# The z projection of a hybrid decoder layer computed with tokens as the stationary operand, and its silu turned by TensorE

## The reference, cut to what matters

```python
z, xbc, dt_raw, q, k, v, gate_logits = jnp.split(u @ w_in, IN_SPLITS, axis=-1)
xbc = silu(causal_dwconv(xbc, ssm_conv_w, ssm_conv_b))
xs, bm, cm = split(xbc)                       # 4096, 8*128, 8*128 channels
y = ssd_chunked(xs, dt, a, bm, cm) + d_skip * xs
y = y.reshape(b, s, 8, 512) * silu(z).reshape(b, s, 8, 512)
y = y * rsqrt(mean(y * y, axis=-1) + eps)     # one mean per group of 512 channels
```

## Time and profile before

| | |
|---|---|
| median of three runs | 1941.22 us |
| the profiled execution's own time | 1941.04 us |
| its span, first to last instruction | 1938.9 us |
| TensorE (PE) busy | 1921.0 us, 99% |
| weight loads (PEld) busy | 1634.6 us, 84% |
| VectorE (DVE) busy | 1265.0 us, 65% |
| ScalarE (ACT) busy | 1084.6 us, 56% |
| DMA queues, share of 16 engines | 61% |
| granted TensorE clock | 0.999 of full |

### The profile page before, as it was taken

The page is one execution under the profiler, slowest core; times in us unless marked ns, Lnnn a source line. Parts: engine busy times, 40 slices in busy tenths (PEclk is TensorE's granted clock), DMA queues, the critical chain, the costliest instruction groups (busy, mean ns, idle before and its releaser), DMA issues.

```text
span 1938.9 us, 28968 instructions
## 1 busy us (share of the span) xinstructions
PE 1921.0 (99%) x10273; PEld 1634.6 (84%) x10273; DVE 1265.0 (65%) x1534; ACT 1084.6 (56%) x1474; POOL 33.5 (2%) x80
## 2 busy tenths in 40 slices
PE   8999999999999999999999999999999999999998
PEld 7888888888887878888888888888888888888886
DVE  6777788777868975544454555776776666744454
ACT  6567756676556764444344445666666666534443
POOL 1000000000000100000000000000000000000000
PEclk9999999999999999999999999999999999999999
DMA  7766676666654437666666565666666656665564
GB/s 222 209 186 173 196 205 176 192 174 204 197 154 135 133 122 217 193 188 196 195 193 195 175 228 195 197 187 186 191 189 194 187 184 187 192 200 192 194 195 141
DMA packets 294134, 362.05 MB, mean 187 GB/s; under 512 B 10864, under 2 KB 217776, under 8 KB 292656
## 3 DMA queue, kind: packets, MB, share of 16 engines
q1 hardware_dynamic: 294064, 361.12, 61.0%
HBM read 358.91 MB, written 2.16 MB: 186 GB/s over the span
## 4 chain that ended last, share of the span: by engine, by line
PE 97%; DVE 1%; ACT 1%; issue 0%; DMA 0%; DVEq 0%; SPq 0%; POOLq 0%; POOL 0%; ACTq 0%
PE ps L1373 35%; PE ps L1375 18%; PE ps L1358 13%; PE ps L1359 13%; PE ps L1360 13%; PE ps L1561 1%; PE ps L1489 1%; PE ps L1502 1%; PE ps L1513 0%; PE ps L1562 0%; PE ps L1550 0%; PE ps L1406 0%; DMA par<-params 0%; DVE lo L847 0%; ACT hi L437 0%
## 5 line engine op out<-in xcount | busy, mean ns | idle before, releaser
L847 DVE TENSOR_TENSOR lo<-raw,hi 128x1024 fp32r<-128x1024 f32 x658 | 801.6, 1224 | 520.7 <-ACT hi L437 515.1
L1373 PE MATMUL ps<-uHL,hi 128*128 128x512 f32 x2960 | 1042.3, 396 | 1.3 <-DVE uHL L859 1.0
L437 ACT ACTIVATE hi<-raw 128x1024 fp32r<-128x1024 f32 x658 | 688.9, 1055 | 519.3 <-PE ps L1360 386.0
L1375 PE MATMUL ps<-uHL,lo 128*128 128x256 f32 x2960 | 829.1, 280 | 0.0
L1373 PEld LDWEIGHTS ps<-uHL,hi 128*128 128x128 f32 x2960 | 554.9, 187 | 131.7 <-issue 5.0
L1375 PEld LDWEIGHTS ps<-uHL,lo 128*128 128x128 f32 x2960 | 559.9, 189 | 0.1
L1360 PE MATMUL ps<-hi,aL 128*128 128x512 f32 x384 | 149.6, 390 | 0.0
L1360 PE MATMUL ps<-hi,hL 128*128 128x512 f32 x352 | 137.0, 389 | 0.0
L1359 PE MATMUL ps<-lo,hH 128*128 128x512 f32 x352 | 137.0, 389 | 0.0
L1358 PE MATMUL ps<-hi,hH 128*128 128x512 f32 x352 | 137.0, 389 | 0.0
L442 ACT ACTIVATE hb<-ps 128x512 f32<-128x512 f32 x92 | 54.7, 595 | 124.1 <-PE ps L1375 124.1
(11 more groups left out here) (190 smaller groups left out, 1644.8 us busy)
## 6 DMA issues: line engine op xcount, KB each, us to landing
raw<-w_in SPq DMA_DIRECT2D x266, 512.0 KB, 4.3
raw<-w_ffn_in SPq DMA_DIRECT2D x176, 512.0 KB, 3.7
raw<-w_ffn_out SPq DMA_DIRECT2D x88, 512.0 KB, 4.3
raw<-w_ssm_out SPq DMA_DIRECT2D x64, 512.0 KB, 4.3
raw<-w_attn_out SPq DMA_DIRECT2D x32, 512.0 KB, 4.3
raw<-w_o SPq DMA_DIRECT2D x32, 512.0 KB, 4.3
rows_b<-cum_rows SPq DMA_DIRECT2D x8, 1024.0 KB, 6.6
x_tok<-x SPq DMA_DIRECT2D x4, 512.0 KB, 6.8
```

The costliest lines, as they stand in the source:

```text
L437: act.activation(hi[:, s % SLOTS, :], raw[:, s % SLOTS, :], ACT.Copy).then_inc(hi_ready, 1)
L847: ve.tensor_tensor(lo[:, s % SLOTS, :], raw[:, s % SLOTS, :], hi[:, s % SLOTS, :].bitcast(F32), ALU.subtract).then_inc(lo_ready, 1)
L1373: pe.matmul(ps[:, pair + c, :], w_hi, uHL[:, kk].rearrange("p a n -> p (a n)"), start=kk == 0, stop=False)
L1375: last = pe.matmul(ps[:, pair + c, 0:SEQ], w_lo, uHL[:, kk, 0, :], start=False, stop=kk == k - 1)
```

## The change

z changes its form. Units 12 to 19 of each group are now 8 `rows` units, loaded as 2 k-tiles x 512 columns, into pair B; the group has four jobs (A, B, A, B), so every group starts on A and a loop body holds one group. ScalarE applies silu while it reads the two finished banks, with the norm factor as its scale, in two instructions, into `szb` with tokens on the partitions; this stands at unit 2 of the next group, ahead of `silu_conv`. After `y_of`, TensorE turns the eight 128 x 128 blocks of `szb` into banks M and M + 3 (`turn_z`), and VectorE multiplies y by them there. Two `half_keep`, two `scaled` and the silu of 1024 columns go away per group. `turn_x` now waits for the last group's gating instead of its skip.

```diff
-                columns(U_G + 12, d, "in", g * GW + C_Z, KD)
+                half_rows(g, d, 0)
+            def half_rows(g, d, j):
+                for i in range(4 * j, 4 * j + 4):
+                    stream(U_G + 12 + i, d, "in", 2 * i, 2, g * GW + C_Z, W5)
             def group_end(g, d):
-                columns(U_G + 16, d, "in", g * GW + (C_Z + W2), KD)
+                half_rows(g, d, 1)
...
             def silu_gate(k):
-                act.wait_ge(z_scaled, k * 2 + 2)
-                act.activation(szb[:], szb[:], ACT.Silu).then_inc(sz_ready, 1)
+                act.wait_ge(unit_used, k * G_UN + (U_G + G_UN))
+                for t in range(TT):
+                    last = act.activation(szb[:, t, :], ps[:, B + t, :], ACT.Silu, scale=rstd1[:, t:t + 1])
+                last.then_inc(pair_free[B], 1)
+                last = act.sem_inc(sz_ready, 1)
...
                 if u == 2:
+                    silu_gate(k)
                     silu_conv(k)
-                if u == 4:
-                    silu_gate(k)
...
-            def gate_scaled_z(g, odd, it, j):
-                scaled(szb[:, 2 * j:2 * j + 2, :], (A, B)[(5 * odd + 3 + j) % 2], g * 5 + (H_G + 4 + j)).then_inc(z_scaled, 1)
...
             def ssd_gate(k):
-                ve.wait_ge(sz_ready, k + 1)
-                ve.tensor_tensor(y[:], y[:], szb[:], ALU.mult).then_inc(y_gated, 1)
+                ve.wait_ge(z_turned, k + 1)
+                for i in range(2):
+                    out = y[:, 2 * i:2 * i + 2, :].rearrange("p a n -> p (a n)")
+                    last = ve.tensor_tensor(out, ps[:, (M, M + 3)[i], :], out, ALU.mult)
+                last.then_inc(y_gated, 1)
...
                 if not first:
-                    pe.wait_ge(y_skipped, k)
+                    pe.wait_ge(y_gated, k)
...
+            def turn_z(k):
+                pe.wait_ge(sz_ready, k + 1)
+                for i in range(4):
+                    for t in range(TT):
+                        o = (i % 2) * SEQ + t * P
+                        last = pe.transpose(ps[:, (M, M + 3)[i // 2], o:o + P], szb[:, t, i * P:(i + 1) * P], ident[:])
+                last.then_inc(z_turned, 1)
...
                 if u == at[1]:
                     y_of(k)
+                    turn_z(k)
...
-                        columns(U_G + u, g * G_UN, pair, KD, 4 * (u % 4), 4)
+                    elif u < 12:
+                        columns(U_G + u, g * G_UN, (A, B, A)[u // 4], KD, 4 * (u % 4), 4)
+                    else:
+                        rows(U_G + u, g * G_UN, B, U, KD, 2 * (u - 12))
...
-            group(1, 1, 0, lambda u: ssd_after(0, u, older=False))
-            with pe.Fori(1, G // 2) as it:
-                for odd in range(2):
-                    g = it * 2 + odd
-                    group(g, odd, it, lambda u: ssd_after(g - 1, u))
+            group(1, lambda u: ssd_after(0, u, older=False))
+            with pe.Fori(2, G) as g:
+                group(g, lambda u: ssd_after(g - 1, u))
```

More of the change, by code:

```diff
@@ L78 @@
 J_G = 1
-J_X = J_G + 5 * G // 2
+J_X = J_G + 2 * G
 J_Q = J_X + 1
@@ L85 @@
 H_G = 1
-H_X = H_G + 5 * G
+H_X = H_G + 3 * G
 H_Q = H_X + 2
@@ L167, in build @@
         sv, a = place("sv", [P, 6, SEQ], a)
-        szb, a = place("szb", [P, 4, SEQ], a)
+        szb, a = place("szb", [P, TT, GW], a)
         xd, a = place("xd", [P, TT, GW], a)
@@ L231, in build @@
         pv_done, attn_out = sem("pv_done"), sem("attn_out")
-        sv_ready, z_scaled, rows_landed, rows_used = sem("sv_ready"), sem("z_scaled"), sem("rows_landed"), sem("rows_used")
+        sv_ready, z_turned, rows_landed, rows_used = sem("sv_ready"), sem("z_turned"), sem("rows_landed"), sem("rows_used")
         conv_first, conv_done, sz_ready = sem("conv_first"), sem("conv_done"), sem("sz_ready")
@@ L567, in y_squares, with group @@
                 act.activation(ysq[:], y[:], ACT.Square).then_inc(y_squared, 1)
[L569 to L576, removed]
+            def group(g, body):
                 for u in range(G_UN):
                     hi_of(U_G + u, g * G_UN)
[L580 to L583, removed]
+                    if u == 6:
+                        half_keep(A, g * G_UN + (U_G + 4))
+                    if u == 10:
+                        act.wait_ge(pair_free[A], g * 2 + (J_G + 1))
+                        half_keep(B, g * G_UN + (U_G + 8))
+                    if u == 14:
+                        act.wait_ge(pair_free[B], g * 2 + (J_G + 1))
+                        half_keep(A, g * G_UN + (U_G + 12))
                     if u == 7:
@@ L630, in keys_side @@
                     act.activation(act_rows[:], ps[0:SH, M + 1, SEQ:2 * SEQ], ACT.Copy).then_inc(acol_ready, 1)
-            group(0, 0, 0, keys_side)
-            group(1, 1, 0, lambda u: ssd_side(0, u))
-            with act.Fori(1, G // 2) as it:
-                for odd in range(2):
-                    g = it * 2 + odd
-                    group(g, odd, it, lambda u: ssd_side(g - 1, u))
+            group(0, keys_side)
+            with act.Fori(1, G) as g:
+                group(g, lambda u: ssd_side(g - 1, u))
             def gate(dst, pair, done, ready):
@@ L647, in _ @@
                 hi_of(U_X + u, 0)
-                if u == 2:
-                    act.wait_ge(pair_free[A], J_X)
-                    half_keep(B, U_X)
                 if u == 6:
-                    act.wait_ge(pair_free[B], J_X)
                     half_keep(A, U_X + 4)
@@ L1025, in conv_rest, with group @@
                     ve.drain()
-            def gate_scaled_z(g, odd, it, j):
-                scaled(szb[:, 2 * j:2 * j + 2, :], (A, B)[(5 * odd + 3 + j) % 2], g * 5 + (H_G + 4 + j)).then_inc(z_scaled, 1)
-            def group(g, odd, it, body):
+            def group(g, body):
                 for u in range(G_UN):
                     lo_of(U_G + u, g * G_UN)
-                    if u == 2 and not (isinstance(g, int) and g == 0):
-                        gate_scaled_z(g - 1, 1 - odd, it, 1)
                     if u in (6, 10, 14):
-                        conv_scaled((A, B)[(5 * odd + u // 4 - 1) % 2], g * 5 + (H_G + u // 4))
+                        conv_scaled(B if u == 10 else A, g * 3 + (H_G + u // 4))
                     if u == 7:
@@ L1044, in group @@
                     body(u)
-                    if u == 18:
-                        gate_scaled_z(g, odd, it, 0)
             def heads(t):
@@ L1127, in ssd_side @@
                     ssd_mean(k)
[L1129 to L1134, removed]
+            group(0, dt_side)
+            group(1, lambda u: ssd_side(0, u, older=False))
+            with ve.Fori(2, G) as g:
+                group(g, lambda u: ssd_side(g - 1, u))
             LAST_STEPS = dict(inputs=5, low=7, high=8, skip=11, gate=12, sum=13, mean=15)
@@ L1138, in _ @@
                 lo_of(U_X + u, 0)
-                if u == 2:
-                    gate_scaled_z(G - 1, 1, 0, 1)
                 ssd_side(G - 1, u, LAST_STEPS)
@@ L1594, in keys_after, with group @@
                     cumulate()
-            def group(g, odd, it, after):
+            def group(g, after):
                 for u in range(G_UN):
[L1598 to L1601, removed]
+                    if u == 0:
+                        job(A, g * 2 + J_G)
+                    if u == 4:
+                        job(B, g * 2 + J_G)
+                    if u == 8:
+                        job(A, g * 2 + (J_G + 1))
+                    if u == 12:
+                        job(B, g * 2 + (J_G + 1))
                     if u < 4:
-                        columns(U_G + u, g * G_UN, pair + u // 2, KD, 8 * (u % 2), 8, w=P)
+                        columns(U_G + u, g * G_UN, A + u // 2, KD, 8 * (u % 2), 8, w=P)
+                    elif u < 12:
+                        columns(U_G + u, g * G_UN, (A, B, A)[u // 4], KD, 4 * (u % 4), 4)
                     else:
-                        columns(U_G + u, g * G_UN, pair, KD, 4 * (u % 4), 4)
+                        rows(U_G + u, g * G_UN, B, U, KD, 2 * (u - 12))
                     after(u)
-            group(0, 0, 0, keys_after)
+            group(0, keys_after)
             pe.wait_ge(kdup_ready, 1)
             pe.wait_ge(acol_ready, 1)
-            group(1, 1, 0, lambda u: ssd_after(0, u, older=False))
-            with pe.Fori(1, G // 2) as it:
-                for odd in range(2):
-                    g = it * 2 + odd
-                    group(g, odd, it, lambda u: ssd_after(g - 1, u))
+            group(1, lambda u: ssd_after(0, u, older=False))
+            with pe.Fori(2, G) as g:
+                group(g, lambda u: ssd_after(g - 1, u))
             def quarter(s, d, u, pair, n):
```

## The result

The changed kernel takes 1943.43 us (median of 20 runs, 1942.95 to 1944.21); the kernel before, run beside it, 1940.72 us (20 runs, 1940.34 to 1941.35). The ratio is 1.0014, 95% interval 1.0008 to 1.0020: 2.7 us more, a small loss that can be told from nothing over twenty runs, and less than the 0.2% that was set as the bound. Forecast were 1943.9 us and +2.8 us.

A forecast was written before the change was run, and what follows sets the result against it. The prediction took TensorE's issue, busy 99% of the span, as the bound; -5.2 + 0.4 + 7.0 + 0.6 = +2.8 us gave 1943.9 us, +0.14%, range 1939.8 to 1946.3 us.

The forecast's parts named there:

- TensorE's own steps set the time: Whole kernel: TensorE, busy 99% of the span, never idles for another engine in the groups, so what it issues sets the time.
- z in rows form, -5.2 + 0.4 us: 64 z units: 179.3 us in columns form become 174.1 in rows form; slightly longer steps after seven mean_y add 0.4 us.
- turn_z, +7.0 us: Eight transposes behind y_of in each of 8 groups, 0.87 us per eight, bounds 6.4 to 7.1 us.
- 25 us: Estimate for all 64 transposes of turn_z at the Trainium skill's 390 ns each; the kernel would take some 1962 us.
- The steps of the pairs that stay, +0.6 us: Columns pairs from group 1's turn_x on: 544 of 712 take the long step instead of 448; bounds -3.0 to +1.8 us.
- The open half, units 10 and 11: Columns units 10 and 11 of the groups: half of their pairs were counted as taking the long step.
- The three terms of the sum: TensorE's changes: z units in rows form -5.2 + 0.4, turn_z's transposes +7.0, steps of remaining columns pairs +0.6 us.
- ScalarE and VectorE: Per group ScalarE drops 0.9 us and VectorE 2.6 us, nothing on the path; `lo` of unit 6 stays ahead of TensorE.
- All long and full price: Rival, chance 0.12: all remaining pairs in the groups get the long step, transposes cost full price; +4.3 us, 1945.4 us.
- All short: Rival, chance 0.11: all remaining columns pairs in the groups get the short step; -0.8 us, 1940.3 us.
- the FFN turns long: Rival, chance 0.05: about 1380 FFN pairs fall into the long step after the last transposes; +9.2 us, 1953 us.
- Form makes no difference: Rival, chance 0.02: z units keep their present 179.3 us in rows form, so +8.0 us, 1949 us.

## Why the prediction was right, step by step

**TensorE's own steps set the time.** Right. No idle time of TensorE in the groups; putting 18.8 of the 20.7 us back that VectorE was relieved of changed nothing.

**z in rows form, -5.2 + 0.4 us.** Measured from the two traces, unit 12 to the next unit 0, with mean_y in it: 22.30 us after in each of seven groups; before 22.64 in the three with short steps, 22.91 in the two with both kinds, 23.07 in the two long ones, and in group 0 21.8 against 22.6. Together -4.6 us, where -4.8 was forecast.

**turn_z, +7.0 us.** 8 x 0.85 = 6.8 us in the trace, 6.99 us by doubling. Right within 3%. The Trainium skill (VectorE: DVE Perf Modes, The three transpose paths) has 390 ns for one in bf16; in a row here each holds the next matmul back by 0.11 us, and the row's own duration is 273 ns (tile szb below). 25 us was never near.

**The steps of the pairs that stay, +0.6 us.** The pattern that was read from groups 4 and 7 came true in every group: long behind the rows units, short behind the root, long behind turn_x. The open half, units 10 and 11, came out long. That is 600 long pairs of 712 where 544 were forecast, +1.0 us by the count. Read from start to start, the pairs that stay take 295.8 us where they took 295.0, +0.8 us: a stretch behind turn_z or behind rows units is a little shorter than an equally long-stepped one was (the 16 pairs behind turn_z 5.73 us, behind y_of before 5.75; unit 0 2.81 us against 2.82). The terms then give -4.6 + 6.8 + 0.8 = +3.0 us, and the stage length is +2.93.

**The number.** The three terms of the sum missed by +0.2, -0.2 and +0.2 us, which partly cancel. And the measured +2.7 us holds something that was in no term: a run's time is 2.1 us more than the span from the first to the last instruction in all runs of the kernels with z in columns form, but 1.7 us in all runs of those with z in rows form (in the profiled executions 1941.04 and 1938.9 us before, 1942.95 and 1941.2 us after). The forecast took 2.1 us for both. Why it is less, no run here shows. So the mechanism and the size are right, but that sum and result agree to 0.1 us is luck. The absolute forecast, 1943.9 us, is 0.5 us high because the three runs that it started from were (1941.22 us; 1940.72 over twenty).

**ScalarE and VectorE.** The rows on szb in the changed kernel answer to the earlier trace rows; the timelines of DVE and of PE to the earlier trace rows.

```profile
L1556 PE MATMUL ps<-ident,szb x64: 272/273/329, 135.3 to 564.9; 128*128 128x128 f32 x64
L545 ACT ACTIVATE szb<-ps,rstd x16: 680/686/690, 103.6 to 535.3; 128x512 f32<-128x512 f32 x16
```
```profile
177.96 1.23 DVE L842 TENSOR_TENSOR lo<-raw,hi 128x1024 fp32r<-128x1024 f32 x1 [1.70 <-ACT hi L441]
...
202.23 1.28 DVE L1070 TENSOR_TENSOR y<-ps,y 128x512 f32<-128x512 f32 x2
```
```profile
182.80 0.40 PE L1359 MATMUL ps<-uHL,hi 128*128 128x512 f32 x1
```

The silu out of PSUM takes 0.686 us (0.684 forecast). `lo` of unit 6 ends at 179.19 and TensorE begins the unit at 182.80, 3.6 us later where 3.3 were before. The gate starts at 202.23, 4.4 us after the transposes are through. These are as forecast. ScalarE's busy time fell by 5.1 us on the page, where 8 x 0.9 = 7 were forecast; it is on no path, so it cost nothing.

**The rivals.** "All long and full price" came nearest: all stretches but those behind the root are long. "All short" and "the FFN turns long" didn't happen. "Form makes no difference" is refuted by the kernel without turn_z; the Trainium skill's 2.5 ns per matmul (TensorE: Matmul & The Clock Gate, Back-to-back issue gap), which it gives for a single matmul and not for a stream with a weight load before each, isn't what these matmuls of 512 columns take beside their columns, which is 13 ns in rows form.

## What to carry to other kernels

When one engine is busy without a gap, a change is the sum of what it adds to and takes from that engine's own order, and start-to-start distances of like instructions in the same trace price it to a few tenths of a us; durations of pipelined instructions do not. A transposition of a result costs TensorE 0.11 us per 128 x 128 block here, so moving a product to the form with fewer matmuls pays only if no transposes come with it: 4.4 us came back and 6.8 went. Where the same instructions run at two speeds, look for what changes between the stretches: here the order of four matmuls, in the kernel before, gained 3.1 us, where the whole change lost 2.7. And compare two traces of the same code first: a level may fall otherwise with no instruction changed.

## What was not expected of the hardware

A pair of matmuls (512 columns, then 256, each with its own weights) runs at 346.7 or at 353.3 ns from start to start at a granted clock of 0.999, and keeps its level until other matmuls come between. In the groups the level that follows is the same in every group or repeats with two or three, and changes with one transpose more or an order; in group 0 and in the attention stage it differed between traces with the same order of TensorE's instructions. The rows form (three times 512 columns) has one level, 226.7 ns each. With both 512-column matmuls first and both 256-column ones behind, there is one level too, 348.3 ns per pair. What makes the long level is open; that it is weight loads which come a little late, no run here shows.
